# The first 32 key tiles of a product-key expert layer read whole for U as for V, by SP's queue

## The reference, cut to what matters

```
h[t, e] = gelu(dot(x[t], U[e]))          for the 128 experts of token t
y[t]    = sum over e of gate[t, e] * h[t, e] * V[e]
```

## Time and profile before

| | |
|---|---|
| median of 3 runs | 3085.14 us (3076.94 to 3086.59) |
| span of the profiled execution (first to last instruction) | 3083.2 us; no other time of it is recorded |
| mean granted TensorE clock | 0.951 |
| busy over the whole span | PE 88%, weight loads 64%, DVE 68%, ACT 37%, POOL 32% |
| DMA, mean over the span | 269 GB/s; 827.89 MB |
| the expert layer's stretch, 1829 us to the end | 1254 us, 41% of the span |

### The profile page before, as it was taken

The page is one execution under the profiler, slowest core; times in us unless marked ns, Lnnn a source line. Parts: engine busy times, 40 slices in busy tenths (PEclk is TensorE's granted clock), DMA queues, the critical chain, the costliest instruction groups (busy, mean ns, idle before and its releaser), DMA issues.

```text
span 3083.2 us, 34652 instructions
## 1 busy us (share of the span) xinstructions
PE 2723.6 (88%) x12212; PEld 1969.0 (64%) x12212; DVE 2111.9 (68%) x2870; ACT 1146.2 (37%) x1980; POOL 988.0 (32%) x567
## 2 busy tenths in 40 slices
PE   9999999999999999999999975666666877669997
PEld 8888788888887888999889872222223433235433
DVE  5687665555564545445566688887888887679877
ACT  5455555555553335445665530000002330034000
POOL 0021000000000000000000038777778777878864
PEclk9999999999999999999999997898999888988999
DMA  7444455555555555453354459999999999999997
GB/s 271 151 155 164 173 178 183 189 190 190 190 177 191 184 185 183 178 182 135 127 191 173 164 228 415 419 409 410 408 417 411 416 407 402 420 376 383 409 402 305
DMA packets 123586, 827.89 MB, mean 269 GB/s; under 512 B 22167, under 2 KB 22183, under 8 KB 23855
## 3 DMA queue, kind: packets, MB, share of 16 engines
q0 software_dynamic: 79392, 510.36, 40.8%
q1 hardware_dynamic: 43920, 313.73, 28.5%
q10 hardware_dynamic: 144, 2.10, 0.2%
HBM read 892.00 MB, written 4.22 MB: 291 GB/s over the span
## 4 chain that ended last, share of the span: by engine, by line
PE 58%; POOL 14%; DMA 11%; DVE 9%; issue 5%; ACT 3%; DVEq 0%; SPq 0%; ACTq 0%
PE ps L608 49%; POOL rows L1324 14%; DMA rows<-peer_u,arena 7%; PE ps L1230 2%; DMA rows<-peer_v,arena 2%; DMA rows<-peer_v 2%; DVE arena L2449 2%; PE ps L1241 2%; DVE WL L506 1%; PE ps L716 1%; ACT arena L1800 1%; DVE arena L209 1%; DVE arena L202 1%; PE ps L916 0%; DVE arena L203 0%
## 5 line engine op out<-in xcount | busy, mean ns | idle before, releaser
L506 DVE SCALAR_TENSOR_TENSOR WL<-ring,PA,WH 128x512 fp32r<-128x512 f32 x896 | 633.1, 753 | 461.7 <-ACT WH L490 445.1
L1241 PE MATMUL ps<-rows,rstd 128*128 128x512 f32 x1164 | 629.6, 694 | 300.1 <-DMA rows<-peer_v,arena 216.9
L2449 DVE CUSTOM_DVE_ANT_0 arena<-rows,arena 128x2048 f32<-128x2048 f32 x256 | 586.9, 2293 | 155.7 <-DMA rows<-peer_u,arena 128.9
L1241 PEld LDWEIGHTS ps<-rows,rstd 128*128 128x128 f32 x1164 | 245.8, 221 | 670.5 <-issue 371.9
L1324 POOL DMA_INDIRECT rows<-peer_v,arena x256 | 484.0, 1891 | 196.8 <-DVE arena L2449 73.4
L489 ACT ACTIVATE WH<-ring,PA 128x512 fp32r<-128x512 f32 x448 | 324.2, 724 | 550.1 <-PE ps L608 401.7
L1324 POOL DMA_INDIRECT rows<-peer_u,arena x256 | 451.4, 1763 | 165.7 <-DVE WL L506 85.9
L608 PE MATMUL ps<-WH,HH 128*128 128x512 f32 x1120 | 442.8, 395 | 4.0 <-DVE WL L506 4.0
L608 PE MATMUL ps<-WH,HL 128*128 128x512 f32 x1120 | 438.0, 391 | 0.0
L608 PE MATMUL ps<-WL,HH 128*128 128x512 f32 x1120 | 437.9, 391 | 0.0
L490 ACT ACTIVATE WH<-ring,PA 128x512 fp32r<-128x512 f32 x448 | 317.2, 708 | 0.0
(11 more groups left out here) (367 smaller groups left out, 3538.0 us busy)
## 6 DMA issues: line engine op xcount, KB each, us to landing
ring<-stream SPq DMA_DIRECT2D x292, 1024.0 KB, 4.8
rows<-peer_v POOLq DMA_DIRECT2D x32, 1024.0 KB, 15.4
rows<-peer_u,arena POOLq DMA_INDIRECT x256, 14.8
rows<-peer_v,arena POOLq DMA_INDIRECT x256, 15.0
arena<-xT SPq DMA_DIRECT2D x4, 512.0 KB, 9.3
bias_rows<-bias_scratch POOLq DMA_DIRECT2D x1, 2048.0 KB, 10.5
arena<-xT ACTq DMA_DIRECT2D x1, 2048.0 KB, 9.5
arena<-memT POOLq DMA_DIRECT2D x1, 2048.0 KB, 10.7
```

What stands on the lines that cost most here:

```text
L506: ins = nc.vector.scalar_tensor_tensor(out=half_tile(WL, u)[:, s], in0=raw_half(u)[:, s], scalar=gain[d], in1=half_tile(WH, u).bitcast(f32 ...
L1241: last = mm(ps[:, 4 * tt + q, :], DIAG[:, k % DIAGS, :], rows[:, SLOTS[n % ROWS], q * CH:(q + 1) * CH], start=n == mine[0], stop=n == ends[q])
L2449: ins = V.tensor_tensor_reduce(out=JUNK, in0=rows[:, SLOTS[n % ROWS], :], in1=HN[:, tt, :], scale=1.0, scalar=0.0, op0=ALU.mult, op1=ALU.a ...
```

## The change

- U rows of experts with ia < 32 are no longer gathered either: one index (IDU) serves both tables. The 32 tiles of U are read whole, as entries "turned" of ROW_ORDER: 2 in each of the groups 0 to 7, 4 in each of 8 to 11. V rows beside U: 9 a group in groups 1 to 7 and 12 to 15, 5 in 8 to 11, none in 0 (119 in place of 135); 137 are left for after ROW_LAST, where PE takes one in 8 (18 in all) and the dense entries start at the 10th.
- For a turned tile PE transposes it (16 of 128x128, in four parts), ACT copies each part out of PSUM, and PE multiplies it with the turned, normalised x [2048, 256 tokens] (16 matmuls of 256 columns). Two tiles make a pair, whose 512 columns ACT squares, DVE makes a polynomial of, ACT takes the tanh of and DVE completes to a gelu. The tile's parts 2 and 3 are done at the next V row or turned entry (finish_u).
- The one-hot batches now need only gates, not hidden values. They all stand in groups 12 to 15, one in 3.5 U rows, and DVE multiplies their result into the dense hidden values (weigh_dense) where ACT copied it.
- Experts are chosen once in 12 U rows from the 11th on (CHOOSE_AT). The gate's weighting moves from finish to weigh. The first of the sums over PSUM for tt = 0 goes.
- Before the rows PE turns the normalised x (32 transposes), ACT copies it out (8 of 512 columns).
- All 64 whole tiles are issued by SP on its own queue, each with a wait for its slot, on the semaphores of the old weight ring; POOL passes over them. SP issues V's after its wait for the last group's hidden values and the load of the last gain.

The diff, cut to its core (the rest renames semaphores and moves buffers):

```diff
 N_DENSE = 32
-LEAD = 9
 BATCH = 16
 BATCHES = P // BATCH
-DENSE_FROM, TAIL, SHARED = 35, 8, 3
-RING_OF = (16, 32)
+STREAMED = 292
+DENSE_FROM, TAIL, SHARED = 10, 8, 3
+LEADS = [0] + [9] * 7 + [5] * 4 + [9] * 4
+U_TILES = [2] * 8 + [4] * 4 + [0] * 4
+U_AFTER = {0: (), 2: (5, 12), 4: (1, 5, 9, 13)}
+PART_AT = (0, 6144, 12288, 10240)
+U_PARTS = (0, 2, 1, 3)
+U_ORDER = [8 * part + i for part in U_PARTS for i in range(8)]
...
-N_LEAD = LEAD * (GROUPS - 1)
+N_LEAD = sum(LEADS)
...
-    if m < DENSE_FROM:
-        return m % 5 == 4
+    if m < N_LAST - TAIL:
+        return m % 8 == FIRST_V1 % 8
     return m in (N_LAST - TAIL + 1, N_LAST - TAIL + 3)
...
         ROW_ORDER.append(("u", _g, _j))
-        if _g and LEAD * _j // PEER_K != LEAD * (_j + 1) // PEER_K:
+        if LEADS[_g] * _j // PEER_K != LEADS[_g] * (_j + 1) // PEER_K:
             ROW_ORDER.append(("v", *V_ORDER[_v]))
             _v += 1
-assert _v == N_LEAD
+        if _j in U_AFTER[U_TILES[_g]]:
+            ROW_ORDER.append(("turned", _d, 0))
+            _d += 1
+assert _v == N_LEAD and _d == N_DENSE
...
 for _tab, _g, _j in ROW_ORDER:
-    _by = "pe" if _tab == "dense" or _tab == "v" and by_matmul(PEER_K * _g + _j - N_LEAD) else "dve"
-    _count[_by] += 1
+    _by = "turned" if _tab == "turned" else "pe" if _tab == "dense" or _tab == "v" and by_matmul(PEER_K * _g + _j - N_LEAD) else "dve"
+    _count[_by] += 4 if _by == "turned" else 1
     ROW_DONE.append((_by, _count[_by]))
...
+for _n, (_tab, _g, _j) in enumerate(ROW_ORDER):
+    if _tab == "turned":
+        FINISHED_AT[_g] = next(n for n in range(_n + 1, ROW_LAST) if ROW_ORDER[n][0] in ("v", "turned"))
+SQUARE_AT, POLY_AT, TANH_AT, GELU_AT = ({FINISHED_AT[2 * p + 1] + later: p for p in range(N_DENSE // 2)} for later in (2, 5, 8, 11))
...
-for _b in range(BATCHES):
-    BATCH_AT[ROW_AT["u", 9 + _b // 2, 3 + 8 * (_b % 2)]] = (0, _b)
-    BATCH_AT[ROW_AT["v", *V_ORDER[N_LEAD + 4 * _b + 3]]] = (1, _b)
-TURN_AT = {ROW_AT["u", 8, 3]: 0, ROW_LAST: 1}
+for _n in range(TT * BATCHES):
+    _g, _j = divmod(12 * PEER_K + 8 + 7 * _n // 2, PEER_K)
+    BATCH_AT[ROW_AT["u", _g, _j]] = divmod(_n, BATCHES)
+TURN_AT = {ROW_AT["u", 12, 4]: 0, ROW_AT["u", 14, 0]: 1}
...
+U_ROWS = [(g, j) for g in range(GROUPS) for j in range(PEER_K)]
+CHOOSE_AT, GATE_AT, WEIGH_AT = ({ROW_AT["u", *U_ROWS[10 + 12 * (g - EARLY) + later]]: g for g in range(EARLY, GROUPS)} for later in (0, 3, 6))
+WEIGH_AT.update({ROW_AT["u", 0, 3 + 2 * g]: g for g in range(EARLY)})
...
+    if _tab in ("dense", "turned"):
+        _name, _tiles = f"weight_tile_in_slot{_tiles % RING}", _tiles + 1
...
+        def slot_free(eng, n):
+            if n < 4:
+                eng.wait_ge(split, 2 * (N_TILES - 3 + n))
+            elif n < ROWS:
+                eng.wait_ge(used, 2 * (N_TILES - (2 if n < 6 else 1 if n < 8 else 0)))
+            else:
+                by, count = ROW_DONE[n - ROWS]
+                eng.wait_ge(sem({"dve": "rows_dve", "pe": "rows_pe", "turned": "raw_turned"}[by]), count)
...
+            def whole_rows(n, table, ia):
+                name, landed = ROW_IN[n]
+                slot_free(sp, n)
+                sp.wait_ge(sem(name), landed - 16)
+                sp.dma_start(rows[:, SLOTS[n % ROWS], :], table[ia * PEER_KEYS:(ia + 1) * PEER_KEYS, :]).then_inc(sem(name), 16)
...
+            for n, (tab, d, _) in enumerate(ROW_ORDER):
+                if tab == "turned":
+                    whole_rows(n, u_tab, U_ORDER[d])
             sp.wait_ge(sem("hidden"), GROUPS)
             sp.dma_start(GROW, bass.AP(gfin_row.tensor, 0, [[0, P], [1, D]])).then_inc(sem("gfin_in"), 16)
+            for n, (tab, c, _) in enumerate(ROW_ORDER):
+                if tab == "dense":
+                    whole_rows(n, v_tab, c)
...
+            pe.wait_ge(sem("xhat_dve"), TT + 1)
+            for b in range(8):
+                if b == 4:
+                    pe.wait_ge(sem("scores_kept"), 8)
+                for k in range(2):
+                    for tt in range(TT):
+                        last = nc.tensor.transpose(ps[:, b, k * TOK + tt * P:k * TOK + (tt + 1) * P], HN[:, tt, (2 * b + k) * P:(2 * b + k + 1) * P], ident)
+                last.then_inc(sem("turned"), 1)
...
+            def turn_u(n, d, part):
+                q = 4 * d + part
+                if part == 0:
+                    pe.wait_ge(sem(ROW_IN[n][0]), ROW_IN[n][1])
+                if q >= 2:
+                    pe.wait_ge(sem("transposes_kept"), TT + q - 1)
+                else:
+                    pe.wait_ge(sem("norm_leading"), 8 * len(TURNED) + 8)
+                for k in range(4):
+                    at = (4 * part + k) * P
+                    last = nc.tensor.transpose(ps[:, 6 + q % 2, k * P:(k + 1) * P], rows[:, SLOTS[n % ROWS], at:at + P], ident)
+                last.then_inc(sem("raw_turned"), 1)
...
+            def u_products(d, part):
+                q = 4 * d + part
+                if d % 2 == 0 and part == 0 and d >= 4:
+                    pe.wait_ge(sem("gelu_done"), 1 + d // 2 - 1)
+                pe.wait_ge(sem("transposes_kept"), TT + q + 1)
+                for k in range(4):
+                    kt = 4 * part + k
+                    last = mm(ps[:, 4 + d // 2 % 2, d % 2 * TOK:(d % 2 + 1) * TOK], UT[q % 2][:, k, :], HNT[kt // 8][:, kt % 8, :],
+                              start=kt == 0, stop=kt == KD - 1)
+                last.then_inc(used, 1)
...
+            def finish_u(n, d):
+                u_products(d, 0)
+                turn_u(n, d, 2)
+                u_products(d, 1)
+                turn_u(n, d, 3)
+                u_products(d, 2)
+                u_products(d, 3)
...
-                pe.wait_ge(sem("hidden"), PEER_H * (tt + 1))
-                if tt:
-                    pe.wait_ge(sem("cleared_then_first_sum"), 2)
-                for k, v in enumerate((IAF, IBF, HI)):
-                    last = nc.tensor.transpose(ps[:, (6, 2)[tt], k * P:(k + 1) * P], v[:, tt, :], ident)
+                pe.wait_ge(sem("gates_ready"), 1 + PEER_H * (tt + 1))
+                pe.wait_ge(sem("transposes_kept"), TT + 4 * N_DENSE)
+                for k, v in enumerate((IAF, IBF, GB)):
+                    last = nc.tensor.transpose(ps[:, 6 + tt, k * P:(k + 1) * P], v[:, tt, :], ident)
...
+                elif tab == "turned":
+                    if turned:
+                        finish_u(*turned)
+                    turn_u(n, g, 0)
+                    turn_u(n, g, 1)
+                    turned = n, g
                 elif tab == "v" and (ROW_DONE[n][0] == "pe" or n >= FIRST_SHARED):
                     gathered_rows(n, g, k)
                     k += 1
+                    if turned:
+                        finish_u(*turned)
+                        turned = None
...
-                if n < 4:
-                    pool.wait_ge(split, 2 * (N_TILES - 3 + n))
...
-                elif n >= ROWS:
-                    by, count = ROW_DONE[n - ROWS]
-                    pool.wait_ge(sem(f"rows_{by}"), count)
-                if tab == "dense":
-                    pool.dma_start(rows[:, SLOTS[n % ROWS], :], v_tab[g * PEER_KEYS:(g + 1) * PEER_KEYS, :]).then_inc(sem(f"row_in{n % ROWS}"), 16)
+                if tab in ("dense", "turned"):
                     continue
+                slot_free(pool, n)
...
-                    in_offset=bass.IndirectOffsetOnAxis(ap=(IDU if tab == "u" else IDV)[:, at:at + 1], axis=0),
-                    bounds_check=last_row, oob_is_err=False).then_inc(sem(f"row_in{n % ROWS}"), 16)
+                    in_offset=bass.IndirectOffsetOnAxis(ap=IDU[:, at:at + 1], axis=0),
...
+            for b in range(8):
+                act.wait_ge(sem("turned"), 8 * len(TURNED) + b + 1)
+                A(HNT[b // 4][:, 2 * (b % 4):2 * (b % 4) + 2, :], ps[:, b, :].rearrange("p (k t) -> p k t", t=TOK), ACT.Copy).then_inc(sem("norm_leading"), 1)
...
-                per = RING_OF[tt] // BATCH
-                if b >= per:
-                    act.wait_ge(sem("dense_h"), n + 1 - per)
-                at = BATCH * (b % per)
+                if n >= 2:
+                    act.wait_ge(sem("dense_h"), n - 1)
+                else:
+                    act.wait_ge(used, 2 * N_TILES + 4 * N_DENSE)
+                v = ONE_HOT[n % 2]
...
-            def keep_dense_h(tt, b):
...
+            def keep_turned_u(d, part):
+                q = 4 * d + part
+                act.wait_ge(sem("raw_turned"), RAW_TURNED + q + 1)
+                if q >= 2:
+                    act.wait_ge(used, 2 * N_TILES + q - 1)
+                A(UT[q % 2], ps[:, 6 + q % 2, :].rearrange("p (k i) -> p k i", i=P), ACT.Copy).then_inc(sem("transposes_kept"), 1)
...
+            def square_u(p):
+                act.wait_ge(used, 2 * N_TILES + 8 * p + 8)
...
+                A(dense_hidden(p), ps[:, 4 + p % 2, :], ACT.Square, scale=math.sqrt(0.044715)).then_inc(sem("squares"), 1)
+            def tanh_u(p):
+                act.wait_ge(sem("gelu_poly"), 1 + p + 1)
```

(67 more changed lines are left out.)

116 lines of the change are left out of this document (74 added, 42 removed).

## The result

The changed kernel takes 3146.74 us (median of 5 runs, 3140.79 to 3164.47), the kernel before 3083.74 in the same comparison: a ratio of 1.021 [1.0193, 1.0228], 63 us slower. The forecast was 3075, its range ended at 3118.

The account below looks back on a forecast made before the run. DMA engines, by bytes, were taken to bound the U part (1829 to 2737 us), other engines close behind. U part -26 and V part +16 gave -10 us on a span of 3083.2: 3075 us, range 3030 to 3118.

Parts of the forecast that it names:

- Groups 8 to 11: U part: PE leads with 55.0 us a group, 220 in all against DVE's 203; 223 us with the choices.
- ACT ... so nothing for its work; its waits are in the rival: U part: ACT's added copies, squares and tanh's, some 100 us on an engine busy 0.07 to 0.27, cost nothing.
- the rival: U part: PE becomes the bound at turned tiles, priced at clock 0.87; +34 with the V part, 3119 us; chance 0.23.
- the argument against it: U part: more PE work per burst and less than half its idle time left keep the slow clock away.
- Groups 12 to 15: End of the U part: POOL needs 4 x 50.7 = 203 us, DVE 200, PE 46 a group.
- Group 0: Start of the U part: 51 us of DVE; turning the normalised x costs nothing, hidden where PE is idle.
- Groups 1 to 7: U part: 405 us, set by POOL's gathers beside DVE's rows and 5.6 us of slot waits at each choice.
- Bytes: Software queue falls to about 401 MB; the rival that bytes decide after all: -84, 3001 us, chance 0.05.
- V part: From 2737 us on: 339 us at 405 GB/s plus 26 of tail, 365; taken as 362, 16 more than before.
- a full ring at the turn: Start of the V part: 12 slots of rows already landed would give 353 us in place of 365.
- SP's queue: V part: SP issuing tiles saves POOL 19 us of issue and 43.3 us of waits, worth nothing at DMA share 1.00.
- The signs named: Right if U part's DMA share is 0.90 to 0.95 and DVE busy 0.93 or more, V part near 362 us.

Follow-up runs that it names:

- after: The changed kernel itself, with all its orders as first written: median 3146.74 us, ratio 1.021; its profiled execution took 3164.47 us.
- e1: Changed kernel, but ACT issues each diagonal (gate matrix of a V row) one V row ahead: 3111.03 us, ratio 1.0088.
- e4: Changed kernel, but all 64 whole tiles issued by POOL in the order of rows, none by SP: 3150.92 us, ratio 1.0225.
- e3: Changed kernel, but the gates of groups 0 to 2 weighed at U rows 10, 12 and 14, not 4, 6 and 8: 3138.54 us, ratio 1.0181.
- e12: e11, but DVE's dot product of a U row runs over 1024 of 2048 columns, bytes unchanged: 3038.43 us, ratio 0.9855.
- e5: e1, but U gathers fetch all rows again, while U's 32 tiles are still read: 3183.92 us, ratio 1.0336.
- e11: e1 plus e3, turned tiles and V rows moved, diagonals two rows ahead, later gelu, group 0's last turned tile finished before the first V row: 3084.82 us, ratio 1.0003.
- e2: Changed kernel, but only 5 of a turned tile's 16 products computed, copies and hand-overs kept: 3105.54 us, ratio 1.0074.

## Why the prediction was wrong

Step by step, with the profile of after (its 18 us over the median included).

- **The step that failed** is "Groups 8 to 11: 5 x 3.55 + 4 x 9.3 = 55.0 us" of PE, taken as the length of these groups, 223 us with the choices. The work was nearly right: PE is busy 213.66 us there, a turned tile takes 9.8 us for 9.3. The length was 252. The sum of one engine's work put its hand-overs with ACT, four per tile and one more per V row in fixed orders, at nothing, without a reason in the sum. PE's waits for diagonals are 37.3 us there and the groups came out 29 us over the forecast. e1 shows it: with the same work and another order of ACT's diagonals the four groups take 218 us, 5 under the forecast.
- **"ACT ... so nothing for its work; its waits are in the rival"**: true of its work, but the waits were no part of the forecast's own range. The place, "a turned tile, where PE and ACT hand over eight times", was nearly right, and so was its test, "groups 8 to 11 over 58 us each with PE waiting for ACT's copies or at a clock under 0.94": they took 63 on average. But PE waited for diagonals (37.3 us), which stand behind copies and squares on ACT; its products waited 1.3 us for copies in the whole U part. And the price was wrong: it was worked out from a clock of 0.87, and the clock was 0.95 to 0.97 in groups 1 to 11. That the rival's 63.2 us for a group of 8 to 11 is what they took is luck. By the trace the argument against it, that more work for PE lifts the clock, held in groups 8 to 11 (0.86 to 0.97), and I let the whole rival shrink with it. The rule in the Trainium skill (TensorE: Matmul & The Clock Gate, the section on oscillation), named in the prediction, agrees with this: the clock rose. It says nothing of what PE's waits for ACT cost.
- **Groups 12 to 15**, forecast 203 (DVE and POOL), took 241, and 224 and 230 in e4 and e3, which keep these orders. PE was mis-sized: 46 us a group at 3.55 a V row and 3.5 a batch; e1, without PE's waits for diagonals, still has PE busy 201.10 of its 217 us, 50 a group. In e4 the 36 V rows take 139.2 us, 3.87 each. PE had more work there than DVE (185.67 us), but e12 shows that it did not set the 217 alone. The waits for diagonals add some 8 us (225 in e4), and the rest up to 241, 16 us, is the clock of 0.88 in that one execution.
- **Group 0**, forecast 51, took 58: the 7.7 us of the weighing behind ACT's copies and table load. "Nothing" for these copies named idle PE as the cover, but not who stood behind them on ACT. e3 gets 12 us of the group back and about 8 of the whole.
- **Groups 1 to 7**: 405 forecast, 409 measured, but the reason given, POOL's gathers beside rows and its slot waits, is not borne out. e12 takes 105 us off POOL's busy time there and gains 10 us. The number is right in part by luck; what sets these groups stays open.
- **Bytes**: 401 MB forecast for the software queue, 400.93 measured. That the bytes alone do not decide was right as well; that they still count e5's 73 us show.
- **V part**: 362 forecast, 372. The kernel was at 407 and 393 GB/s in its two stretches, 136.7 MB in 345 us, 396 on average, where I had 339 us at 405: 6 us. The tail is 27 for 26. Nothing was to be had from a full ring at the turn, of which I had put 3 us into the number.
- **SP's queue**: "worth nothing", e4 confirms within 4 us.
- **The signs named** for a right forecast: the DMA share of the U part came out at 0.90, the low end of "0.90 to 0.95", but DVE was busy 773 of 960 us, 0.81 and not "0.93 or more".

The terms miss by 7 + 4 + 29 + 38 + 10 = 88 us of the span. In the medians it is 72 (3147 against 3075). Of the 63 us of the loss e1's order gives back 36 and e3's about 8. With tiles and V rows moved, the wait of the first V row and the gelu steps as well, all of it comes back within measurement (e11). What stays in e11 is an even exchange: by the table its U part takes 887 us against 907 before, its V part 368 against 346.

Not settled: what the same care about order would give the kernel before. It has 41 us of waits for diagonals of its own, at a DMA share of 1.00 to 1.01, and e1's edit was not tried in it; so e11 says that the turned tiles can be had at no loss, not what they are worth. Not settled either: why the V part stays at some 395 GB/s where the earlier trace rows has 405 at the same share. More of its gathers have holes per tile read, but no run took that apart.

## What to carry to other kernels

Where engines meet in fixed orders, the busiest engine's sum of work is a lower bound and not a forecast of the time: for every new hand-over, list what the other engine has queued ahead of it, and issue the small thing that a busy engine will want (here a diagonal of 0.4 us) one item early. Price a risk by the waits that were found for it, not by a nearby number such as the clock. And before counting bytes as saved time, check which engine is next: here, in the best order found (e11), 34 MB fewer bought 20 us in the U part, and all of it went into the V part.

## What the runs showed of the hardware

- A share is not a rate. With holes in the gathers of U and V groups 1 to 7 ran at 363 GB/s with a DMA share of 0.94 (after), with holes in V's alone at 412 with 1.01 and, in e5, at 399 with 0.97: 386 per unit of share against 408 and 411.
- The granted clock of groups 8 to 11 rose when PE got more work, from 0.86 before (busy 176.63 of 234 us) to 0.97 after (213.66 of 252) and 0.99 in e1 (208.39 of 218), and was 0.91 in e2 (151.34 of 218). The busy share alone does not give it: 0.75 stands beside 0.86 before, 0.69 beside 0.91 in e2. And it differs between executions with the same orders of PE and ACT: groups 12 to 15 had 0.88, 0.92 and 0.95 in after, e3 and e4, with the same six waits for diagonals.
- POOL's gathers get shorter when DVE's instructions do: the mean POOL time of one in groups 1 to 7 is 308.68/171 = 1.81 us in e11 and 204.12/171 = 1.19 us with DVE's rows halved (e12).
